# Head preparation with unscaled queries, modulation chunks redistributed, and the scan factors on one engine

## What is computed

```python
def rms_norm(x, g):
    xf = x.astype(jnp.float32)
    y = xf * lax.rsqrt(jnp.mean(xf * xf, axis=-1, keepdims=True) + EPS)
    return (y * g.astype(jnp.float32)).astype(x.dtype)

def attend(q, k, v, scale):
    s = jnp.einsum("bqkgd,blkd->bkgql", q, k).astype(jnp.float32) * scale
    p = jax.nn.softmax(s, axis=-1).astype(v.dtype)
    return jnp.einsum("bkgql,blkd->bqkgd", p, v)

# mixer_q, mixer_kv, for each of the two kinds of heads
q_mla = rms_norm(q_mla, lp["g_qn_mla"])
k_mla = rms_norm(jnp.concatenate([k_nope, k_rope], axis=-1), lp["g_kn_mla"])
q_mla = jnp.concatenate([q_mla[..., :64], apply_rope(q_mla[..., 64:], rope_mla)], axis=-1)   # the 256 tokens of x only

# layer: the modulation
mod = (silu_c @ lp["w_mod"] + lp["b_mod"])[:, None, :]

# second block, for each direction, group of heads and chunk of 32 tokens, b the running sum of the log gates
s = (q * exp(b - ref)) @ (k * exp(ref - b)).T      # inside a chunk
q_dec = q * exp(b);  k_dec = k * exp(b_last - b)   # between chunks
```

## Time and profile before

| | us |
|---|---|
| median of 3 runs | 2200.82 (2198.29 to 2203.59) |
| profiled execution | 2197.82, its span 2196.0 |
| head preparation, layer 0 | 150.7 to 234.8 |
| attention, layer 0 | 234.8 to 388 |
| head preparation, layer 1 | 1114.8 to 1175.5 |
| attention, layer 1 | 1175.5 to about 1252 |
| scans of mixer AB | about 1757 to 1809 |
| scans and groups of mixer C | about 1890 to 2145 |

### The profile page before, as it was taken

How to read it: one execution, slowest core, us unless ns; L and a number is a source line. 1 busy time by engine, 2 the same in 40 slices (tenths; PEclk the granted TensorE clock), 3 DMA queues, 4 the chain that set the end, 5 groups by cost and what they waited for, 6 DMA issues and landing times. The chain is left out here.

```text
span 2196.0 us, 31241 instructions
## 1 busy us (share of the span) xinstructions
PE 1964.1 (89%) x12007; PEld 1646.1 (75%) x12007; DVE 1225.0 (56%) x1841; ACT 942.2 (43%) x1387; POOL 213.4 (10%) x216
## 2 busy tenths in 40 slices
PE   5988899999998999999977999899988967799886
PEld 3864576688877888887844799799887865789885
DVE  3338556343346555423565456677444576678885
ACT  3323444332324444312434555566336452566751
POOL 3000000000000222200000000022100030111310
PEclk9989999999998999999987999899998988899988
DMA  8226546333231222323310056455563323433331
GB/s 287 89 79 218 166 136 216 93 86 107 81 115 58 96 96 96 121 100 105 110 44 1 19 164 182 147 173 173 190 222 108 116 71 103 134 116 120 111 120 73
DMA packets 262663, 265.88 MB, mean 121 GB/s; under 512 B 6278, under 2 KB 230896, under 8 KB 262560
## 3 DMA queue, kind: packets, MB, share of 16 engines
q1 hardware_dynamic: 257008, 247.22, 35.3%
q0 software_dynamic: 4832, 15.06, 2.1%
q10 hardware_dynamic: 720, 2.17, 0.2%
HBM read 263.33 MB, written 1.10 MB: 120 GB/s over the span
## 5 line engine op out<-in xcount | busy, mean ns | idle before, releaser
L1627 DVE TENSOR_TENSOR weights_fine<-region,weights_coarse 128x2048 fp32r<-128x2048 f32 (+3 forms) x187 | 431.9, 2310 | 403.9 <-ACT weights_coarse L1055 403.1
L1055 ACT CAST weights_coarse<-region 128x2048 fp32r<-128x2048 f32 (+3 forms) x187 | 358.9, 1919 | 370.9 <-PE bank L466 353.2
L464 PE MATMUL bank<-normed_coarse,weights_coarse 128*128 128x512 f32 (+1 forms) x1088 | 367.7, 338 | 14.4 <-DVE normed_fine L1733 9.1
L465 PE MATMUL bank<-normed_fine,weights_coarse 128*128 128x512 f32 (+1 forms) x1088 | 366.7, 337 | 0.0
L466 PE MATMUL bank<-normed_coarse,weights_fine 128*128 128x512 f32 (+1 forms) x1088 | 366.6, 337 | 0.0
L464 PEld LDWEIGHTS bank<-normed_coarse,weights_coarse 128*128 128x128 f32 x1088 | 207.5, 191 | 37.8 <-issue 13.6
L465 PEld LDWEIGHTS bank<-normed_fine,weights_coarse 128*128 128x128 f32 x1088 | 207.6, 191 | 21.3
L466 PEld LDWEIGHTS bank<-normed_coarse,weights_fine 128*128 128x128 f32 x1088 | 207.5, 191 | 21.4
L464 PE MATMUL bank<-x_turned_coarse,weights_coarse 128*128 128x256 f32 x616 | 185.3, 301 | 34.4 <-DVE weights_fine L1627 30.4
L465 PE MATMUL bank<-x_turned_fine,weights_coarse 128*128 128x256 f32 x616 | 182.3, 296 | 0.0
L466 PE MATMUL bank<-x_turned_coarse,weights_fine 128*128 128x256 f32 x616 | 181.8, 295 | 0.0
(11 more groups left out here) (265 smaller groups left out, 3781.0 us busy)
## 6 DMA issues: line engine op xcount, KB each, us to landing
region<-in_w_mod SPq DMA_DIRECT2D x48, 1024.0 KB, 5.1
region<-in_w_up SPq DMA_DIRECT2D x44, 1024.0 KB, 4.9
region<-in_w_in_c SPq DMA_DIRECT2D x30, 1024.0 KB, 5.0
region<-in_w_in_ab SPq DMA_DIRECT2D x20, 1024.0 KB, 5.1
region<-in_w_in SPq DMA_DIRECT2D x32, 512.0 KB, 4.3
region<-in_w_down SPq DMA_DIRECT2D x16, 1024.0 KB, 4.9
region<-in_w_in SPq DMA_DIRECT2D x14, 1024.0 KB, 5.0
region<-in_w_in SPq DMA_DIRECT2D x16, 384.0 KB, 3.4
```

Of the source, the lines that this page charges most:

```text
L464: nc.tensor.matmul(o, sc, mc, start=first, stop=False)
L465: nc.tensor.matmul(o, sc, mf, start=False, stop=False)
L1055: nc.scalar.copy(w_co[:, p, 0:size], raw_w[:, s, 0:size]).then_inc(coarse_ready, 1)
L1627: nc.vector.tensor_tensor(w_fi[:, p, 0:size], raw_w[:, s, 0:size], w_co[:, p, 0:size].bitcast(F32), ALU.subtract).then_inc(fine_ready, 1)
```

## The change

It has five parts, of which the first three belong together.

1. Raw queries. Queries are no longer multiplied by the reciprocal root. The root's reciprocal goes to a table `q_scale`, per head and token, and enters attention twice: as `scale` of the exponential on ACT, and in a new 128x1 multiplication on DVE that turns the negated maximum into the exponential's bias, in every one of the 96 steps of layers 0 and 1. Keys are still multiplied by it.
2. Gains. For the part that isn't rotated the gain becomes the `scale` of ACT's copy out of the transposes, taken from a table `gain_cols` that is made at the start of the program by 8 more transposes on PE and 8 small copies on ACT, before ACT takes the roots of the first norm. For the rotated part the gain is multiplied into the rotation tables, by POOL, four operations per layer. Rotation now comes before the scaling.
3. Order of head preparation. ACT, no longer DVE, copies the latent products of the keys out. `raw` has two buffers. The grouped half is finished in its own item; both sums, both roots and one reciprocal stand together. The zeros in `qT` are written by POOL, behind the rotation tables, and PE waits for them before attention.
4. Modulation chunks: one per item of head preparation in place of two (8 in place of 16), and in attention 8 per 16 steps in place of 6 (32 in place of 24).
5. Scans: POOL's four operations per scan move to DVE, in front of, between and behind its own.

```diff
-MOD_FILLS = [16 * t + i for t in range(4) for i in (1, 3, 6, 8, 11, 13)]
+MOD_FILLS = [16 * t + i for t in range(4) for i in (1, 3, 5, 7, 8, 10, 12, 14)]
...
             def heads_prep(l):            # PE
...
-                for s in range(len(tiles)):
-                    if s:
-                        gqa_transposes(tiles[s - 1][0])
+                for s, (kind, t) in enumerate(tiles):
+                    copied = following
                     if l == 0:
                         mod_chunk()
                     if s + 1 < len(tiles):
-                        products(*tiles[s + 1])
-                    mla_transposes()
-                    if l == 0:
-                        mod_chunk()
-                gqa_transposes(tiles[-1][0])
+                        following = products(*tiles[s + 1])
+                    mla_transposes(kind, t, raw[s % 2], copied)
+                    gqa_transposes(kind, t)
...
             def attend(l):
                 evacuated()
+                pe.wait_ge(zeros_ready, GQA_KV * (4 + 2 * l))
...
+            for l in range(DEPTH):        # PE, at the start
+                ps = begin()
+                for j, (kind, which) in enumerate(GAIN_AT):
+                    at, d = GAIN_AT[kind, which], GQA_DIM if which else MLA_QK
+                    mm = nc.tensor.transpose(ps[0:d, j * P:(j + 1) * P], g_rows[:, l, at:at + d], ident[:, :])
+                end(mm)
...
+                if l == 0:                # ACT
+                    act.wait_ge(gains_ready, 1)
+                raw_of(0)
+                squares_of(0)
                 for s, (kind, t) in enumerate(tiles):
...
+                    if s + 1 < len(tiles):
+                        raw_of(s + 1)
+                    roots_of(kind)
+                    if s + 1 < len(tiles):
+                        squares_of(s + 1)
                     turned_mla(kind, t)
+                    turned_gqa(kind, t)
...
-                        nc.scalar.activation(p_sb[:, J % 2, 0:nk], src, ACT.Exp, bias=small[:, 48 + J % 4:49 + J % 4],
+                        nc.scalar.activation(p_sb[:, J % 2, 0:nk], src, ACT.Exp, bias=small[:, at + J % 4:at + 1 + J % 4],
+                                             scale=q_scale[:, i // 16, i % 16:i % 16 + 1] if scaled else 1.0,
...
+                for s, (kind, t) in enumerate(tiles):      # DVE
+                    roped = t < ROPED_TILES
+                    sums_of(kind)
...
+                        m = rotate_mla(s)
...
+                        m = rotate_gqa(s)
...
                     seen_next(rsh_ready)
+                    if kind == "q":
+                        step(nc.vector.reciprocal(q_scale[:, t, :], small[:, 16:32]))
                     else:
+                        link(nc.vector.reciprocal(small[:, 64:74], small[:, 16:26]))
+                        heads = raw[s % 2].rearrange("p (h d) -> p h d", h=HEADS)
+                        nc.vector.tensor_tensor(heads, heads, over_heads(small[:, 64:72], HEADS, MLA_QK), ALU.mult).then_inc(nrm_ready, 1)
...
                     if chunk:
                         mod_chunk(chunk)
...
+                        if scaled:
+                            link(largest)
+                            largest = nc.vector.tensor_tensor(small[:, 88 + J % 4:89 + J % 4], small[:, 48 + J % 4:49 + J % 4],
+                                                              q_scale[:, i // 16, i % 16:i % 16 + 1], ALU.mult)
...
             def factors(d, scan, q, k):
...
                 dve.wait_ge(exps_ready, 5 * scan + 4)
+                nc.vector.tensor_tensor(last, last, k, ALU.mult).then_inc(kd_ready, 1)
                 step(nc.vector.tensor_tensor(mid, mid, q, ALU.mult))
                 nc.vector.tensor_tensor(inv, inv, k, ALU.mult).then_inc(qe_ready, 1)
+                dve.wait_ge(exps_ready, 5 * scan + 5)
+                nc.vector.tensor_tensor(run, run, q, ALU.mult).then_inc(qd_ready, 1)
```

## The result

The changed kernel took 2184.82 us (median of 4 runs, 2183.67 to 2187.35), the kernel before 2201.84 in the same comparison: ratio 0.9926, 95% interval 0.9909 to 0.9943, so 12.5 to 20 us faster. A second comparison gave 0.9918 (0.9901 to 0.9934). The forecast was 2182.

The account below looks back on a forecast made before the run. PE was taken to bound the whole, with its waits deciding the touched stages. Start +2.5, head preparation −12.5 and −7.6, attention +13, scans −3 and −10 gave −17.6, about 2183.2, stated as 2182 us; range 2166 to 2194.

Follow-up runs that it names:

- c5: The changed kernel with its new tables behind the work regions and the gains' transposes and copies moved from the start into layer 0's head preparation; ratio 0.9937.
- b1: The changed kernel with ACT's roots of an item ahead of the next item's raw copies in head preparation; 2160.76 us, ratio 0.9805.

## What to carry to other kernels

Where two engines wait for each other in every item, write down which wait of the one stands ahead of which result for the other: the order of two calls on ACT was worth 24 us here, more than the change itself. A step that is moved off a chain still waits if the PSUM bank that it needs is given free behind the chain (1.75 us a query item here); and giving it free sooner helps only as far as the next wait (0.28). When tables are added ahead of a region that DMAs write, look whether the loads slow down, and put the tables behind the region if they do. Before a stage's time in one profile is explained, look at the same stage in other kernels that don't differ there.

## What I had not expected of the hardware

- 1 MB loads into regions moved by 320 bytes, to 64 past a multiple of 256, took 5.3 us instead of 5.1, and the kernel before, with nothing but that, took 0.17% (0.06 to 0.29) longer.
- With a wait of 3.0 to 3.3 us in each key item three items ran at clocks of 0.96, 0.75 and 0.84, in c5 at 0.84, 0.83 and 0.81; with 1.59 in each (b1) at 1.00.
- With the same instructions and waits, head preparation of layer 1 took 47.9 to 53.1 us in eight profiles, at clocks of 0.91 to 0.82.
- The same 3160 matmuls, with the same waits for other engines as far as the views show, took 700 and 706 us in two kernels that differ only in stages ahead of them. What makes that difference stays open.
